# Two attention layers and a banded, convolving block on one core: turned value products, divided probabilities and a separate ring for the compress weights

## What is computed

```python
# a hybrid layer (twice)
p = split_columns(rms_norm(x, pre_g) @ w_in + b_in)
o_sb  = stick_breaking_attention(...)            # 4 heads of 128
o_nsa = native_sparse_attention(...)             # compressed, selected, window branch
o_fox = forgetting_attention(q, k, v, log_f)     # z = q k / sqrt(d) + cum[q] - cum[k]
o_mla = latent_attention(...)                    # q_nope k_nope + q_rot k_rot, 64 rotary channels
x = x + rms_norm(concat(o * silu(gate)) @ w_out, post_g)
# the second half (once)
aq, ak, av, bu, bg, cq, ck, cv = split(rms_norm(x, norm1_g) @ w_in_2)
out_a = dilated mixture, 8 heads of 64           # scores + log(number of patterns that see the key)
out_b = silu(layer_norm(causal depthwise conv, 31 taps, of bu * sigmoid(bg)))
out_c = banded attention, 16 query and 2 key heads of 64, with sinks
x = x + concat(out_a, out_b, out_c) @ w_out_2
x = x + (silu(h2 @ w_gate) * (h2 @ w_up)) @ w_down
```

## Time and profile before

| what | value |
|---|---|
| time, median of three executions | 2049.43 us (2046.37 to 2050.29) |
| the profiled execution | 2047.95 us |
| its span, first to last instruction | 2046.3 us |
| mean granted TensorE clock | 0.997 |
| busy in the span: PE, PEld, DVE, ACT, POOL | 99%, 84%, 55%, 46%, 4% |
| chain that ended last | PE 90%, DVE 4%, ACT 2% |
| moved by DMA | 360.80 MB, 176 GB/s |

### The profile page before, as it was taken

How to read it: one execution, slowest core, us unless ns; L and a number is a source line. 1 busy time by engine, 2 the same in 40 slices (tenths; PEclk the granted TensorE clock), 3 DMA queues, 4 the chain that set the end, 5 groups by cost and what they waited for, 6 DMA issues and landing times.

```text
span 2046.3 us, 28056 instructions
## 1 busy us (share of the span) xinstructions
PE 2015.8 (99%) x10474; PEld 1714.3 (84%) x10474; DVE 1127.8 (55%) x1318; ACT 932.3 (46%) x1216; POOL 76.1 (4%) x124
## 2 busy tenths in 40 slices
PE   9999999999999999999999999999999999999998
PEld 7889988888889998888888777888888888888886
DVE  5474555656566454654756885644454554444443
ACT  5355444444454543444554435544444444443442
POOL 3000000001100000000300100000000000000000
PEclk9999999999999999999999999999999999999999
DMA  8574455565665444666554434566666666656663
GB/s 264 164 256 124 132 168 169 175 197 160 207 205 189 133 146 147 181 200 192 153 161 135 150 109 142 178 192 189 191 188 191 185 190 189 190 180 215 202 202 110
DMA packets 187753, 360.80 MB, mean 176 GB/s; under 512 B 13169, under 2 KB 19872, under 8 KB 187392
## 3 DMA queue, kind: packets, MB, share of 16 engines
q1 hardware_dynamic: 182832, 345.62, 54.8%
q0 software_dynamic: 4816, 13.76, 2.4%
HBM read 357.23 MB, written 2.10 MB: 176 GB/s over the span
## 4 chain that ended last, share of the span: by engine, by line
PE 90%; DVE 4%; ACT 2%; DVEq 1%; DMA 1%; issue 1%; ACTq 0%; POOL 0%; POOLq 0%; SPq 0%
PE psum L571 24%; PE psum L573 23%; PE psum L572 23%; PE psum L579 3%; PE psum L581 3%; PE psum L582 3%; DVE wl L529 1%; DVE conv_y L789 1%; PE psum L935 1%; PE psum L661 1%; PE psum L647 1%; PE psum L636 1%; DMA raw<-in_w_small_dram 1%; ACT wh L522 1%; PE psum L1141 1%
## 5 line engine op out<-in xcount | busy, mean ns | idle before, releaser
L529 DVE TENSOR_TENSOR wl<-raw,wh 128x1024 fp32r<-128x1024 f32 (+2 forms) x672 | 797.6, 1197 | 706.8 <-ACT wh L522 698.8
L522 ACT ACTIVATE wh<-raw 128x1024 fp32r<-128x1024 f32 (+2 forms) x672 | 689.9, 1036 | 863.0 <-PE psum L573 702.0
L571 PE MATMUL psum<-wh,xh 128*128 128x512 f32 (+2 forms) x1600 | 623.0, 389 | 5.6 <-DVE wl L529 4.7
L573 PE MATMUL psum<-wh,xl 128*128 128x512 f32 (+2 forms) x1600 | 615.7, 385 | 0.0
L572 PE MATMUL psum<-wl,xh 128*128 128x512 f32 (+2 forms) x1600 | 615.4, 385 | 0.0
L571 PEld LDWEIGHTS psum<-wh,xh 128*128 128x128 f32 x1600 | 301.1, 188 | 69.0 <-DVE wl L529 8.3
L573 PEld LDWEIGHTS psum<-wh,xl 128*128 128x128 f32 x1600 | 301.1, 188 | 59.3
L572 PEld LDWEIGHTS psum<-wl,xh 128*128 128x128 f32 x1600 | 301.4, 188 | 56.9
L571 PE MATMUL psum<-wh,mh 128*128 128x512 f32 x376 | 148.5, 395 | 7.5 <-DVE wl L529 4.3
L573 PE MATMUL psum<-wh,ml 128*128 128x512 f32 x376 | 147.1, 391 | 0.0
L572 PE MATMUL psum<-wl,mh 128*128 128x512 f32 x376 | 147.0, 391 | 0.0
(11 more groups left out here) (357 smaller groups left out, 1545.5 us busy)
## 6 DMA issues: line engine op xcount, KB each, us to landing
raw<-in_w_in_dram SPq DMA_DIRECT2D x264, 512.0 KB, 4.3
raw<-in_w_out_dram SPq DMA_DIRECT2D x96, 512.0 KB, 3.6
raw<-in_w_gate_dram SPq DMA_DIRECT2D x88, 512.0 KB, 3.6
raw<-in_w_up_dram SPq DMA_DIRECT2D x88, 512.0 KB, 3.6
raw<-in_w_down_dram SPq DMA_DIRECT2D x80, 512.0 KB, 3.9
raw<-in_cmp_w_dram SPq DMA_DIRECT2D x16, 512.0 KB, 3.9
raw<-in_w_small_dram SPq DMA_DIRECT2D x16, 336.0 KB, 3.7
bias<-in_b_in_dram POOLq DMA_DIRECT2D x18, 256.0 KB, 3.8
```

What stands on the lines that cost most here:

```text
L522: act.activation(wh[:, n % SPLIT_SLOTS, 0:k, 0:unit.n], raw[:, n % RAW_SLOTS, 0:k, 0:unit.n], ACT.Copy).then_inc(hi_done, 1)
L529: dve.tensor_tensor(out=wl[:, n % SPLIT_SLOTS, 0:k, 0:unit.n], in0=raw[:, n % RAW_SLOTS, 0:k, 0:unit.n], in1=wh[:, n % SPLIT_SLOTS, 0:k, 0 ...
L571: pe.matmul(o, ah_[:, kt, tok], hi_w, start=first, stop=False)
L573: ins = pe.matmul(o, al_[:, kt, tok], hi_w, start=False, stop=last)
```

## The change

**Second half.** Probabilities are divided while they still stand by queries: ACT multiplies each of the eight blocks of `prob2` by its factor, behind the exps and the reciprocal (semaphore `_factor`). The values become the stationary operand, 64 columns wide, and the turned probabilities the moving one; even heads write the lower 64 partitions of the output, odd heads the upper (`value_rows`, `c_values`, `a_values`). The output so comes out turned, and ACT and DVE split it at once (`out_high`, `out_low`). The transposes of `o_c` and `o_a`, `small_out` and the splits after them are gone. `log_count` is split once into `count_hi` and `count_lo` and added by six fp32r products of 512 columns (`a_masks`). The scaling of `av` and the copy in mid 20 go from DVE to ACT. The units of `w_out_2` have another order: 32 units in sixteen slots (2, 1, 4, 1, 4, 1, 3, then seven of 2, then 1 and 1), pairs 2 and 3 last, so that PE first asks for `conv_rows2` in slot 27 (`CONV_SLOT`). The taps are dealt anew by three tables, some inside mids while ACT computes exps. The turning of the final x comes in three stages of four tiles.

**Layers.** Compress weights have four buffers of their own, `cmp_raw`; the first four of their loads go out early, between ring units 16, 18, 20 and 22. Rotary pieces are turned two at a time (six transposes), and the rotary products alternate between the 64-partition halves, with a drain between two groups. The sums of log f are made once, in stage 8, by three fp32 products (`fox_sums`), split into three bf16 parts by DVE, and added to the scores by one bf16 product for each head and block. The compress masks are added by one product in place of eight.

```diff
+TAPS_AT_SLOT = {11: (1,), 12: (1, 1, 1, 1), 14: (1, 1, 1, 1), 16: (1, 1), 19: (1,)}
+TAPS_AT_MID = {10: 1, 12: 1, 14: 3, 15: 2, 16: 1, 17: 2, 18: 1, 19: 2}
+TAPS_IN_MID = {11: 2, 13: 1, 17: 2, 19: 1}
...
+        def load_order():
+            for k, n in enumerate(ring_units):
+                if k in CMP_EARLY:
+                    yield cmp_units[CMP_EARLY.index(k)]
+                yield n
+                if n + 1 in cmp_units[CMP_RAW_SLOTS:]:
+                    yield n + 1
...
+                def fox_sums():
+                    o = st[:, 1280:1280 + T]
+                    for first, which, table in ((True, 0, tri_up[:, :]), (True, 0, None), (False, 1, tri_up[:, :])):
+                        dst = o[:, 0:P] if table is not None and first else o[:, P:T]
+                        ins = pe.matmul(dst, fox_col[:, which, :], one.to_broadcast([P, P]) if table is None else table,
+                                        start=first, stop=True, skip_group_check=True)
...
+                    def rope_product(h, blk):
+                        half = slice(64 * (h // 2), 64 * (h // 2) + 64)
+                        o = st[:, h * T:(h + 1) * T] if blk else st[:, 1024 + h * P:1024 + (h + 1) * P]
+                        pe.matmul(o, qrT[half, h % 2, blk * P:(blk + 1) * P], qrT[half, 2, 0:T if blk else P],
+                                  start=False, stop=False, skip_group_check=True)
+                    for h, blk in ((0, 0), (2, 1), (1, 0)):
+                        rope_product(h, blk)
+                    pe.drain()
+                    for h, blk in ((0, 1), (3, 1), (1, 1), (2, 0), (3, 0)):
+                        rope_product(h, blk)
...
+                    for h, blk, o, n, _ in score_places():
+                        pe.matmul(o, fox_pick[:, h:h + 1].to_broadcast([P, P]), fox_rows[:, 0:n], start=False,
+                                  stop=False, skip_group_check=True)
...
+            def value_rows(parity):
+                return st[64 * parity:64 * parity + 64, 1536:2048].rearrange("p (i t) -> p i t", i=2)
...
+            def c_values(group):
+                for kb in range(TB):
+                    for parity in (0, 1):
+                        o, c0 = value_rows(parity), (1024 + 2 * parity * P if kb else 2 * parity * T)
+                        n = P if kb else T
+                        rhs = probT2[:, c0:c0 + 2 * n].rearrange("p (i t) -> p i t", i=2)
+                        ins = pe.matmul(o[:, :, P:T] if kb else o, cv[:, kb, 64 * group:64 * group + 64], rhs,
+                                        start=kb == 0, stop=kb == 1, skip_group_check=True)
...
+                act.wait_ge(s(name + "_factor"), 1)
+                for blk, base, n in ((0, 1024, P), (1, 0, T)):
+                    for h in range(4):
+                        part = prob2[:, base + h * n:base + (h + 1) * n]
+                        act.activation(part, part, ACT.Copy, scale=factor[:, blk * 4 + h:blk * 4 + h + 1])
...
-            after_signal.update({20: conv_square, 22: conv_rstd})
-            after_unit[CONV_UNIT] = lambda: (conv_silu(), act.drain(), conv_high())
+            after_unit[unit_of_2(25, 1)] = conv_rstd
+            after_unit[unit_of_2(CONV_SLOT, 0)] = lambda: (conv_silu(), act.drain(), conv_high())
...
-                9: lambda: both(lambda: turn_pairs(u, 0), lambda: c_values(0, 4)), 10: lambda: both(lambda: turn_pairs(cqn, 0), lambda: turn_pairs(o_c[0], 2)),
+                9: lambda: both(lambda: turn_pairs(u, 0), lambda: c_values(0)), 10: lambda: turn_pairs(cqn, 0),
```

More of the change, by code:

```diff
@@ L147, in output_slots_2, with passed @@
 def output_slots_2():
[L151 to L161, removed]
+    def passed(g, *pairs, of):
+        return [output_unit("w_out_2", g, pair, of[-1], of[0]) for pair in pairs]
+    early, both = (4, 5, 6, 7), (4, 5, 6, 7, 0, 1)
+    late, last = (0, 1, 2, 3), (2, 3)
+    slots = [passed(0, 4, 5, of=early), passed(0, 6, of=early), passed(0, 7, of=early) + passed(1, 4, 5, 6, of=early),
+             passed(1, 7, of=early), passed(2, 4, 5, 6, 7, of=both), passed(3, 4, of=both),
+             passed(3, 5, 6, 7, of=both), passed(2, 0, 1, of=both), passed(3, 0, 1, of=both),
+             passed(0, 0, 1, of=late), passed(1, 0, 1, of=late), passed(0, 2, 3, of=late),
+             passed(1, 2, 3, of=late), passed(2, 2, 3, of=last), passed(3, 2, of=last), passed(3, 3, of=last)]
+    slots[CONV_SLOT - WIN_SLOTS_2][0].after = "conv_rows2"
     return slots
 CMP_SLOTS = (6, 7)
+CMP_RAW_SLOTS = 4
+CMP_EARLY = (16, 18, 20, 22)
 CMP_ROWS = 2 * 16 + 4
@@ L474, in __init__ @@
                 self.units, self.slots, self.loads, self.once, self.single = units, slots, loads, once, single
[L476 to L484, removed]
+        layer_units = [unit for slot in LAYER_SLOTS for unit in slot]
@@ L486, in in_layer @@
         def in_layer(l):
-            return Place(l * LAYER_UNITS, l * NSLOT, [l * q for q in LAYER_PIECES], l + 1, False)
+            return Place(l * LAYER_UNITS, l * NSLOT, [l * LAYER_LOADS_RING] * RAW_SLOTS, l + 1, False)
         def after(units, slots):
             return Place(LAYERS * LAYER_UNITS + units, LAYERS * NSLOT + slots,
[L492 to L497, removed]
+                         [LAYERS * LAYER_LOADS_RING + units // RAW_SLOTS] * RAW_SLOTS, 1, True)
@@ new lines, in raw_buffer @@
+        def raw_buffer(place, n, unit):
+            if unit.layout == "cmp":
+                j = cmp_units.index(n)
+                loads = (place.once - 1) * (len(cmp_units) // CMP_RAW_SLOTS) + j // CMP_RAW_SLOTS + 1
+                return cmp_raw[:, j % CMP_RAW_SLOTS], cmp_raw_loaded[j % CMP_RAW_SLOTS], 16 * loads
+            k = n if place.single else ring_number[n]
+            return raw[:, k % RAW_SLOTS], raw_loaded[k % RAW_SLOTS], 16 * (place.loads[k % RAW_SLOTS] + k // RAW_SLOTS + 1)
@@ L528, in split_low @@
             k = len(unit.kts)
-            dve.tensor_tensor(out=wl[:, n % SPLIT_SLOTS, 0:k, 0:unit.n], in0=raw[:, n % RAW_SLOTS, 0:k, 0:unit.n],
+            buffer, _, _ = raw_buffer(place, n, unit)
+            dve.tensor_tensor(out=wl[:, n % SPLIT_SLOTS, 0:k, 0:unit.n], in0=buffer[:, 0:k, 0:unit.n],
                               in1=wh[:, n % SPLIT_SLOTS, 0:k, 0:unit.n].bitcast(F32),
@@ new lines, in c_masks, with a_masks @@
+                return ins
+            def a_masks():
+                for part in (count_hi, count_lo):
+                    for bank, m, table in ((0, 2, part[:, 0:T]), (1, 2, part[:, 0:T]), (2, 4, part[:, T:T + P])):
+                        o = st[:, bank * 512:(bank + 1) * 512].rearrange("p (m c) -> p m c", m=m)
+                        ins = pe.matmul(o, ident_r[:, :], over(table, m), start=False, stop=True,
+                                        skip_group_check=True)
+                return ins
```

298 lines of the change are left out of this document (167 added, 131 removed).

## The result

The changed kernel takes 2021.4 us (median of four executions, 2020.23 to 2022.03), the kernel before 2049.86 beside it: a ratio of 0.9861, 95% interval 0.9847 to 0.9876. The profiled execution took 2020.23 us with a span of 2018.6. 2022.5 had been forecast.

The account below looks back on a forecast made before the run. Everything PE issues was taken to cost its full time, plus PE's stops and half clocks behind them. 2047.95 - 7.1 - 7.0 - 12.1 - 12.2 + 13.0 = 2022.55, so 2022.5 us, range 2013 to 2034.

Parts of the forecast that it names:

- Small products of the layers: Rotary turns, log f sums, forgetting and rotary scores and compress masks on PE: -3.55 us a layer, -7.1 for two.
- Compress loads: Slot 7 of both layers: own ring and earlier loads end the stops (4.2 us) and the slow clock behind: -7.0.
- So the clock gives another 1.4 twice: Behind each slot 7 stop, 11 products of 336 columns would take 1.65 us instead of 3.1.
- Rival B: Slot 7: small compress units come late by themselves, ACT did not wait for those loads; +7.0, 2029.5 us; chance .10.
- Values turned: Six value stages: column halves side by side take 1.5 us each instead of 2.65, -6.9 in all.
- Rival A: Value stages: column halves don't overlap or drains eat it, 2.6 us each; +6.6, 2029 us; chance .17.
- Turns and masks: Second half: transposes of `o_c` and `o_a` go, -2.5 us; masks of the dilated mixture in fp32r, -2.7.
- Old stops: Second half: PE's stops, convolved rows included, and the half clock behind those rows go: -12.2 us.
- new stops: Second half: PE waits for early division, scalings and splits in mids, slot 17, conv and the end: +13.0 us.
- the price of the scalings: ACT's eight scalings in each softmax, taken as 2.6 us within the sum for the stops.
- Rival C: ACT's scalings, 48 on PE's path, are slow; decides from .93 us each, at 1.1 gives 2060 us; chance .03.
- D: Second half: new stops half as long as forecast, 2016 us; chance .05.

Follow-up runs that it names:

- run 10: Changed kernel with compress weights still in their own four buffers, but no load issued early: 2021.31 us.
- run 11: Changed kernel with the compress units back in the common ring of four raw buffers, in the old order: 2031.81 us.
- run 1: Changed kernel with the products of the values taken first for all lower 64 output partitions, then all upper, instead of alternating: 2023.09 us.
- run 2: Changed kernel with the values' lower partitions first, then a drain of PE, then the upper ones: 2027.11 us.
- run 9: Changed kernel with the division shared by ACT and DVE in c alone, taps moved later, two of them behind mids 11 and 13: 2010.91 us.
- run 8: Changed kernel with the division shared in c alone, five taps later, and the last quarter of all taps' channels on POOL: 2016.86 us.

## Why the prediction was right

The forecast was a fall of 25.4 us from profiled execution to profiled execution, and 27.7 were measured. Of the 2.3 between them, .4 and .5 are the first two terms below, and 1.1 are the first 50 us and the entry of layer two, which differ between runs of one kernel too and which no term forecast. To that extent the measured time is lower by chance.

**Small products of the layers: -7.1, measured -7.5.** In each layer turns and sums +.24 (+.25 forecast), rotary scores 2.81 to 1.88, -.93 (-.85; the .65 taken for the drain and the mode had no row behind it, 1.88 less the 1.3 of a full overlap leaves .58), forgetting scores -2.88 (-2.85), compress masks -.17 (-.1). The stage of the forgetting scores, where the earlier trace rows answer for the fp32 sums:

```profile
316.49 2.78 PE L1336 MATMUL psum<-fox_kT,fox_qT 128*128 128x256 f32 x16
319.11 0.82 PE L1340 MATMUL psum<-fox_rows,fox_pick 128*128 128x256 bf16 x8
319.77 0.61 PE L672 MATMUL psum<-causal_b,ident_b 128*128 128x128 bf16 x8
```

Eight products start .66 us ahead of the masks, as the .67 taken from other bf16 products had it.

**Compress loads: -7.0, measured -7.5, but of other parts.** The groups of slots 4 to 7 lost 4.32 and 3.22. "So the clock gives another 1.4 twice" was wrong: in layer two of the kernel before the clock stayed full behind the stop of 1.95, and there was a stop of .5 ahead of stage 8 that I had overlooked. Its stretch behind the stop, and that wait in the list of waits over the whole span:

```profile
596.40:599.40 3.00, 2.94 (x16) 2.45 (x17) 2.06 (x3) 2.50 (x3) 0.00 (x0) 1.00 0.82 254
```

```profile
PE psum L1188 <- issue: 0.5, 1, 0.5
```

The rest is that a stop costs some .2 us more, from start to start, than its idle time (2.43 for 2.27). The early loads, half of the reason given, had no part in it (run 10); the ring alone did. Rival B fell with runs 10 and 11.

**Values turned: 1.5 a stage, measured 1.44.** Rival A fell with runs 1 and 2. Turns and masks gave less than forecast: the masks take 1.50 and 1.59 instead of 1.36, so -2.4 for -2.7. The time in which PE was busy fell by 13.5 us in the attention part; forecast were 12.1 and 1.6 for the clock.

**Old stops, new stops: -12.2 and +13.0.** The convolved rows never stop PE by more than .13, and no half clock is left. "The other stops lie before stages 8, 12 and 14" was a wrong reading: only 1.4 us of them lay there, at stage 12. The rest was the 2.89 behind stage 17 and 1.8 in four short stops from 1211 to 1241 us, in the part that the change deals anew. They went too, so the size came out, but no reason had been given for them, and no run isolates what ended them. New idle time, from the rows with a wait: stage 6 .3 (.2 forecast), 8 .8 + .9 (1.7), 12 1.8 + .9 (2.7), 14 1.6 + .9 (2.5), slot 17 1.8 (2.3), conv 1.2 (1.0), the end .8 + .2 + 1.6 (2.6): 12.8 for 13.0. The hand sum of mid 7 and the list of what stands behind what carried it; the price of the scalings was .2 us a softmax too low (2.8 for eight, not 2.6), as the estimate from the Trainium skill, "ScalarE: Activation LUTs", What ACT_TABLE_LOAD costs, had it, which the stop of slot 17, .5 shorter than forecast, about made up for. The stops in the conv slots and at the end agree in size, but no run tests their cause. None of the new stops, up to 1.84 us, was followed by a half clock. Rival C, from .93 us a scaling, fell with the .293 and .398 of the records, and D, stops half as long, with the 12.8.

What the forecast did not say is that the 13 us were not the price of the change but of where the pieces stood: with the same products on PE run 9 takes 9 to 10 us less.

## What to carry to other kernels

When a step moves between two mids, write down for each engine what stands between PE's signal and PE's next wait, splits behind the mid included, and set the sum against the slot; that list told the new stops to a few tenths here. A stop is what the whole list exceeds the slot by, so removing any piece longer than the stop ends it, and the gains of two such removals must not be added. Then look where the freed engine arrives early next: 5.4 of 10.3 us came back at once where DVE had no time left. When a stretch is bound by an engine's total, move work to its gaps or to an engine that is idle and does not slow it.

## What was not expected of the hardware

- PE starts products of one column half past up to three waiting instructions of the other (run 1), so even an order that is not interleaved overlaps when the groups are short; a drain between the halves ends it and costs .4 us beside the lost overlap (3.01 against the 2.6 estimated for all products in turn).
- POOL at work beside DVE lengthened DVE's 256-column taps from 480 to 809 ns and its splits from 1223 to 1444, in the mean of the records that it ran beside (run 8); what POOL took over was hardly won.
- POOL's last drain took 3.17 us in run 8 and 6.75 in all other runs, and the end of the program waits for it.
- The half clock does not follow from the length of a stop alone. Before the change it came behind 2.27 and 3.17 us but not behind 1.95, nor behind the 2.89 us at 1198:

```profile
1198.00:1206.00 8.00, 5.11 (x25) 4.10 (x23) 7.36 (x11) 0.43 (x3) 0.00 (x0) 1.00 0.33 108
```

In the run with one ring there was a third stretch at half clock near 1186 us, behind a stop of 1.80, at the very place where the changed kernel stops for 1.82 and keeps the full clock. What decides it the runs do not tell.
